# A fourth output-projection slice split before the last head's second convolution block, and one combination's low part taken at the end of the first feed-forward group

## The reference

```
hn = rmsnorm(h);  xt, b, c, q, k, v, g = split(hn @ w_in)
conv_out = b * conv3(c * xt)                        # width 512, causal, depthwise
ret_out  = silu(g) * groupnorm(retention(rot(q), rot(k), v))   # 4 heads of 128
h = h + concat(conv_out, ret_out) @ w_out
f = square(relu(rmsnorm(h) @ w_up)) @ w_down        # width 4096
y = rmsnorm(h + f)
```

## Time and profile before

| | |
|---|---|
| time before, median of 3 runs | 1175.36 us (1175.01 to 1176.11) |
| the profiled execution's own time | 1177.58 us |
| its span | 1175.8 us |
| TensorE busy | 1161.0 us (99%) |
| VectorE busy | 931.1 us (79%) |
| ScalarE busy | 548.0 us (47%) |
| GpSimd busy | 379.9 us (32%) |
| granted TensorE clock | 1.00 |

### The profile page before, as it was taken

One profiled execution on the slowest core, in us unless ns is written; L12 is line 12 of the kernel. 1 busy time (PEld: TensorE's weight loads), 2 busy tenths in 40 slices (PEclk: granted clock), 3 DMA queues, 4 the chain that ended last, 5 costly groups with the idle time before them and its releaser, 6 DMA issues.

```text
span 1175.8 us, 20816 instructions
## 1 busy us (share of the span) xinstructions
PE 1161.0 (99%) x6346; PEld 1061.5 (90%) x6346; DVE 931.1 (79%) x1630; ACT 548.0 (47%) x1140; POOL 379.9 (32%) x282
## 2 busy tenths in 40 slices
PE   8999999999999999999999999999999999999998
PEld 6899999999999888979989989988998998998996
DVE  6467796887968754499898898898889889889877
ACT  7544434343254432546435435434534633643556
POOL 3401131112220045344343343343433333334303
PEclk9999999999999999999999999999999999999999
DMA  7631111211121441431021021021012112102204
GB/s 268 185 112 37 41 50 36 65 43 40 49 68 62 144 152 36 152 99 45 28 71 54 18 71 54 27 62 62 27 54 62 40 40 71 54 18 71 62 27 153
DMA packets 99714, 82.66 MB, mean 70 GB/s; under 512 B 9936, under 2 KB 82640, under 8 KB 99680
## 3 DMA queue, kind: packets, MB, share of 16 engines
q1 hardware_dynamic: 99392, 81.47, 22.3%
q10 hardware_dynamic: 288, 0.79, 0.2%
HBM read 70.95 MB, written 11.28 MB: 70 GB/s over the span
## 4 chain that ended last, share of the span: by engine, by line
PE 87%; DVE 6%; DMA 3%; issue 1%; ACT 1%; POOL 1%; SPq 1%; POOLq 0%; DVEq 0%; ACTq 0%
PE pp L2065 27%; PE pp L2067 27%; PE pp L2066 27%; PE pp L2071 1%; PE pp L2072 1%; DMA out<-ncs 1%; DVE wo_lo L1536 1%; PE pp L2085 1%; DMA h<-in_x_prompt 1%; DVE mid_lo L1543 1%; PE pp L2199 1%; PE pp L2188 1%; PE pp L2181 1%; PE pp L2198 1%; DMA xr<-in_x_prompt 0%
## 5 line engine op out<-in xcount | busy, mean ns | idle before, releaser
L1752 DVE TENSOR_TENSOR h<-pp,h 128x512 f32<-128x512 f32 x420 | 267.5, 680 | 6.0 <-PE pp L2067 5.9
L2065 PE MATMUL pp<-do_hi,fo_hi 128*128 128x512 f32 x452 | 177.0, 392 | 2.0 <-DVE fo_lo L1745 2.0
L2067 PE MATMUL pp<-do_hi,fo_lo 128*128 128x512 f32 x452 | 176.4, 390 | 0.0
L2066 PE MATMUL pp<-do_lo,fo_hi 128*128 128x512 f32 x452 | 176.4, 390 | 0.0
L2065 PE MATMUL pp<-mid_hi,fo_hi 128*128 128x384 f32 (+1 forms) x528 | 170.0, 322 | 0.0
L2067 PE MATMUL pp<-mid_hi,fo_lo 128*128 128x384 f32 (+1 forms) x528 | 170.0, 322 | 0.0
L2066 PE MATMUL pp<-mid_lo,fo_hi 128*128 128x384 f32 (+1 forms) x528 | 169.9, 322 | 0.0
L1059 ACT ACTIVATE fo_hi<-fo_flat 128x512 fp32r<-128x512 f32 x124 | 75.7, 625 | 115.9 <-POOL fo_flat L2025 60.9
L1701 DVE TENSOR_TENSOR fo_lo<-fo_flat,fo_hi 128x512 fp32r<-128x512 f32 x124 | 103.2, 854 | 6.3 <-ACT fo_hi L1059 6.3
L2065 PEld LDWEIGHTS pp<-do_hi,fo_hi 128*128 128x128 f32 x452 | 84.8, 188 | 22.8 <-DVE fo_lo L1745 3.1
L2067 PEld LDWEIGHTS pp<-do_hi,fo_lo 128*128 128x128 f32 x452 | 84.9, 188 | 18.1
(11 more groups left out here) (293 smaller groups left out, 2775.5 us busy)
## 6 DMA issues: line engine op xcount, KB each, us to landing
fo_flat<-in_w_up SPq DMA_DIRECT2D x64, 256.0 KB, 2.9
do_raw<-in_w_down SPq DMA_DIRECT2D x49, 256.0 KB, 3.3
i_raw_A<-in_w_in SPq DMA_DIRECT2D x48, 256.0 KB, 3.1
xr<-in_x_prompt SPq DMA_DIRECT2D x8, 512.0 KB, 6.4
do_hraw<-in_w_down SPq DMA_DIRECT2D x15, 256.0 KB, 2.5
tx_raw_T<-tx_parts SPq DMA_DIRECT2D x3, 768.0 KB, 5.9
xt_parts<-fo_hraw SPq DMA_DIRECT2D x9, 256.0 KB, 2.9
xt_raw<-xt_parts SPq DMA_DIRECT2D x3, 768.0 KB, 8.5
```

The costliest lines, as they stand in the source:

```text
L1752: dve.tensor_tensor(h_part(p, q), bank_of(p, q)[:, :], h_part(p, q), ALU.add).then_inc(dve_add, 1)
L2065: pe.matmul(out, a_hi, b_hi, start=start, stop=False, skip_group_check=again)
L2066: pe.matmul(out, a_hi, b_lo, start=False, stop=False, skip_group_check=again)
L2067: return pe.matmul(out, a_lo, b_hi, start=False, stop=stop, skip_group_check=again)
```

## The change

Two edits that have nothing to do with each other.

- **Fourth slice.** On ScalarE, `split_out(6)`, `split_out(7)` and `mid_high(3)` move ahead of `tap0(i, 1)` in the last head. On VectorE, `split_out(6)`, `split_out(7)` and `mid_low(3)` move ahead of `conv(i, 1)`. The loop behind starts with slice 4.
- **Low part of T4.** `xt_lo_part("T4")` moves from between the low parts of A11 and A12 to the end of the first group's down stage, just ahead of `xt_lo_part("T1")`.

No instruction is added or removed, and no semaphore's count changes.

```diff
@@ ScalarE, last head @@
                         split_out(5)
                         mid_high(2)
+                        split_out(6)
+                        split_out(7)
+                        mid_high(3)
                     tap0(i, 1)
                     tap0(i, 2)
@@ ScalarE, behind the heads @@
-            for n in range(3, KT):
+            for n in range(4, KT):
                 split_out(2 * n)
                 split_out(2 * n + 1)
                 mid_high(n)
@@ VectorE, last head @@
                         split_out(5)
                         mid_low(2)
+                        split_out(6)
+                        split_out(7)
+                        mid_low(3)
                     conv(i, 1)
                     evict(i, "b", "C22")
@@ VectorE, up_first @@
                 f_low(0, "A11", F_HI)
-                xt_lo_part("T4")
                 f_low(0, "A12", F_HI)
@@ VectorE, down_group @@
                 add(g, P4, 3)
                 if first:
+                    xt_lo_part("T4")
                     xt_lo_part("T1")
```

## The result

The changed kernel takes 1178.21 us (median of 13 executions, 1176.85 to 1181.96). The kernel before takes 1175.38 us in the same comparison (13 executions, 1174.19 to 1176.97). The ratio is 1.0025 with a 95% interval of 1.0018 to 1.0033, so the change costs about 2.9 us. That is outside the 0.2% in which I put most of the chance, and 0.01 us above the upper end of the range.

What follows compares the result with a forecast made beforehand. TensorE, busy 99% of the span, was taken to bound the kernel. The terms 0 - 1.5 + 2.9 = +1.4 us on a median of 1175.4 gave 1176.8 us, range 1174.3 to 1178.2.

Steps and rivals of the forecast that it cites:

- First edit, 0 us: At slice 3, TensorE's 0.48 us stall goes but is waited again for hw near 441: value 0.
- a longer wait for hw: Sign in the profile after: TensorE waits longer for hw near 441, having arrived 0.48 us earlier.
- Second edit, what it removes, -1.5 us: From P1 to `sample` in group 0, stalls at P2 and the sample's products shrink: gain 1.5 us, between 0.6 and 1.8.
- Second edit, order at the hand-over: From group 0 to group 1, VectorE and GpSimd alternate: T4, sum (1.30 us), T1, sum (1.30 us), S2's part.
- Rivals one and two: At the hand-over VectorE keeps its turn through T1 (1175.5 us, chance 0.20) or also through S2's part (1174.2 us, 0.10).
- Rival four: At the sample's products the small low parts keep losing their turn; only P2's 0.6 us won: 1177.7 us, chance 0.06.
- Second edit, what it adds, +2.9 us: At the hand-over, T4 (1.67 us) and a GpSimd turn (1.30 us) delay S2's part, so P6 starts 2.9 us later.
- with nothing more lost: Behind P6, P5's inputs end about when P6 does, so no loss beyond the 2.9 us wait.
- rival three: Near 427, GpSimd's sum goes ahead of hw; transposes at 441.28 come 1.1 us later: 1177.9 us, chance 0.22.

Runs made afterwards that it cites:

- the filler run: Low part of T4 moved as in the change, slice 3 not, plus 14 unread matmuls ahead of P6, against the kernel before: 1178.61 us, ratio 1.0003.
- the first edit alone: Only slice 3's splits moved ahead of the convolution steps, against the kernel before: 1177.0 us, ratio 1.0000.
- T4 in group 1: T4's low part moved into group 1's list, ahead of sum C22, slice 3 unmoved, against the kernel before: 1175.63 us, ratio 0.9994.
- the earlier load: Loads of the rest of `h` issued ahead of the four small stores, nothing else changed, against the kernel before: 1176.12 us, ratio 0.9997.
- the second edit alone: Only T4's low part moved to the end of group 0, against the kernel before: 1180.34 us, ratio 1.0023.
- T4 ahead of the last adds: Only T4's low part moved, to before the last seven adds of group 0, against the kernel before: 1178.29 us, ratio 1.0008.
- all three: Slice 3 split early, T4's low part in group 1 and the rest of `h` loaded before the stores, against the kernel before: 1174.0 us, ratio 0.9981.

## Why the prediction was wrong, step by step

- **First edit, 0 us.** Right by the measure: 1.0000 alone. The reason was right too: the stall at slice 3 went, and what came behind hung on the store, the load and hw. That the store's landing moves by about 2 us between executions was not in the prediction's sum. A sign that it had named failed too: a longer wait for hw. The changed kernel's profile has none.
- **Second edit, what it removes, -1.5 us.** Right. 1.73 us was won between P1 and `sample` (1.8 was the most that there was); P1's own stall of 1.47 us was called untouched, and it varies by itself.
- **Second edit, order at the hand-over.** Right, instruction by instruction: T4, sum, T1, sum, S2's part. Rivals one and two are out, since VectorE lost both turns in all three profiles with T4 at that place (T1 took 2.85 us in each). In one of the three T4 itself gave way to a sum too, for 0.4 us. Rival four is out, since `sample` no longer waits in the changed kernel, and 0.3 us at most in the other profiles with T4 moved, where it was 0.94.
- **Second edit, what it adds, +2.9 us.** This is the step that failed. The wait is of the forecast size: the gap ahead of P6 grew by 2.72 us. The prediction then wrote that P5's inputs end about when P6 does, "with nothing more lost", and carried the bare wait into the sum. It priced a stall of TensorE at its length. Behind this one the granted clock fell to the lower level, P6 took 1.46 us longer, and the sum was +2.3 us where +1.4 was forecast. In the medians it is +2.83 us. The term was too small by a missing part, the clock, and right in its order and its wait; the filler run removes the missing part alone.
- **What was there to see.** In the kernel before, the longest stall of TensorE in this region was 1.47 us, and the matmuls behind it ran at clock 1.00. So no row of it gave a price for a stall twice as long. An upper bound should have been kept open for that. The range ended at rival three's 1178.2 and left the case out.
- **Rival three.** It gave the time that came out (1177.9), but for another reason. Its mechanism was seen in one of the two profiles that have the first edit with the loads in their old place, and the first edit alone cost nothing in the median.

What stays open: the medians differ by 2.83 us and the rows account for 2.34, which the interval covers. T4's wait for a sum, 0.4 us in one profile and none in another, can be a part of the rest; how often it comes isn't known. How hw and GpSimd's sum are ordered in the timed executions isn't known. The gains of T4 in group 1 and of the earlier load are each too small to be told from nothing by themselves.

## What to carry to other kernels

A stall of the bounding engine isn't priced by its length alone: look in the windows at what the granted clock does behind a stall of that length, and if the trace has none so long, keep a cost for it in the range. Before an instruction is moved to the end of a stage, find which engine is late at that hand-over; a place in the middle of the next stage, where the engine has slack, kept the gain here without the loss in the rows (-1.34 us; the times alone don't settle it). Where two engines exclude each other, an instruction put into the line also costs a turn of the other engine (1.75 us of work delayed S2's part by 2.7 us).

## What the runs showed of the hardware

- TensorE idle for 2.6 us (the changed kernel) and 3.0 us (the second edit alone), after long dense work: the next eight or nine matmuls of 384 columns start 0.32 us apart, with a granted clock of 0.73 and 0.69 in the window, and the level is back at 2.4 GHz about 3 us after they began. Idle for 1.39, 1.47 and 1.65 us (T4 ahead of the last adds; the kernel before; the first edit alone, ahead of the transposes at 444.09): no such thing. Nothing between 1.65 and 2.59 us was measured in such dense work.
- At the kernel's start the level is low too, and there a window's clock of 1.00 can't be trusted. The changed kernel's profile has 0.83 between 10 and 20 us. TensorE had stood idle from 6.79 to 8.52 us and then taken matmuls of 128 and 256 columns before the level fell at 10.1:

```profile
10.00:20.00 10.00, 10.00 (x42) 7.91 (x41) 9.14 (x15) 9.70 (x20) 1.03 (x1) 0.83 1.10 364
```

The same window of the second edit alone says 1.00, and so it does in the kernel before. But the second edit alone has matmuls of 512 columns 0.43 us apart there, the spacing of the lower level (0.23 us at the upper one):

```profile
10.00:20.00 10.00, 10.00 (x41) 8.16 (x40) 9.00 (x15) 9.21 (x20) 0.00 (x0) 1.00 1.10 365
```

```profile
12.51 0.63 PE L2065 MATMUL pp<-wv_hi,hn_hi 128*128 128x512 f32 x1
12.94 0.63 PE L2066 MATMUL pp<-wv_lo,hn_hi 128*128 128x512 f32 x1
13.37 0.63 PE L2067 MATMUL pp<-wv_hi,hn_lo 128*128 128x512 f32 x1
```

By the spacing the slow start ends near 11.7 us in the kernel before, near 13.5 in the changed kernel and near 14.5 in the second edit alone, the filler run and all three. It goes with no edit, and nothing of it can be seen at slice 2, whose last matmul starts at 386.25 us in the changed kernel, against 386.32 before. So the mean clock of a single execution doesn't say whether the hand-over had its slow stretch; only the average over many of one kernel against another does.
- A store of 2 KB, one of four whose 4-byte values lie 512 bytes apart in the output for each partition, took 13 to 17 us here, longer than the 2 MB load behind it (7.9 to 8.7 us). Issued ahead of such stores, the same load took 19.8 to 20.3 us.
